# Dealing the opening of RWKV pairs 2 and 3 out over the chain of pairs 0 and 1, decode softmax in parts, first weights in half slabs

## The reference, cut to what matters

```
h  = LN(ALPHA*x + 0.5*swiglu_a(x))
proj = h @ w_in          # q, k, v of differential attention; r, k, v, decay, rate, gate of RWKV-7
attention: p = softmax(q1 k1) - lam*softmax(q2 k2);  o_da = rmsnorm(p @ v)
rwkv (8 heads of 64): S = S*w + (S @ -kk) b' + v k';  o = S @ r   # a scan over the tokens
o_rw = (groupnorm(o) + sum(r*k*r_k)*v) * gate
h2 = LN(ALPHA*h + [o_da, o_rw] @ w_out)
y  = LN(ALPHA*h2 + 0.5*swiglu_b(h2))
```

## Time and profile before

| | us |
|---|---|
| median of 3 runs | 1348.41 (1346.65 to 1348.88) |
| profiled execution, its own time | 1350.16 |
| its span, first to last instruction | 1348.4 |
| mean granted TensorE clock | 0.976 of full |
| TensorE busy | 1255.0 (93%) |
| VectorE busy | 571.8 (42%) |
| ScalarE busy | 426.2 (32%) |
| GpSimd busy | 105.6 (8%) |
| data moved | 174.77 MB, mean 130 GB/s |

### The profile page before, as it was taken

One profiled execution on the slowest core, in us unless ns is written; L12 is line 12 of the kernel. 1 busy time (PEld: TensorE's weight loads), 2 busy tenths in 40 slices (PEclk: granted clock), 3 DMA queues, 4 the chain that ended last, 5 costly groups with the idle time before them and its releaser, 6 DMA issues.

```text
span 1348.4 us, 29923 instructions
## 1 busy us (share of the span) xinstructions
PE 1255.0 (93%) x12840; PEld 1137.5 (84%) x12840; DVE 571.8 (42%) x814; ACT 426.2 (32%) x652; POOL 105.6 (8%) x98
## 2 busy tenths in 40 slices
PE   6999999999998999997788988798999999999995
PEld 6999999999988988874456544487999999999994
DVE  3323233232436445344543643688533232322354
ACT  4222223222324324425532322423322222222222
POOL 0000000000200100010441021013000000000020
PEclk9999999999999999998997999899999999999998
DMA  5222222233223657554463689441222222222221
GB/s 221 94 84 83 86 89 93 66 90 102 87 100 119 269 177 259 166 186 141 145 213 130 208 285 304 156 166 63 95 94 93 93 93 85 77 71 87 87 63 64
DMA packets 55971, 174.77 MB, mean 130 GB/s; under 512 B 7105, under 2 KB 7362, under 8 KB 47298
## 3 DMA queue, kind: packets, MB, share of 16 engines
q1 hardware_dynamic: 53282, 168.84, 36.6%
q10 hardware_dynamic: 2592, 4.52, 0.9%
HBM read 163.58 MB, written 9.76 MB: 129 GB/s over the span
## 4 chain that ended last, share of the span: by engine, by line
PE 39%; DVE 7%; ACT 3%; SPq 3%; issue 2%; DMA 1%; POOL 0%; DVEq 0%; ACTq 0%
PE acc L273 27%; PE acc L296 3%; SPq L2189 2%; PE acc L1343 1%; PE acc L1526 1%; PE acc L1534 1%; SPq L2181 1%; DVE weights_lo L256 1%; PE acc L889 1%; PE acc L1511 1%; PE acc L1280 1%; DVE y_sum L605 1%; PE acc L1321 1%; ACT map L1461 1%; PE acc L1417 1%
## 5 line engine op out<-in xcount | busy, mean ns | idle before, releaser
L256 DVE TENSOR_TENSOR weights_lo<-weights_raw,weights_hi 128x1024 fp32r<-128x1024 f32 (+2 forms) x186 | 210.9, 1136 | 540.1 <-ACT weights_hi L249 540.0
L273 PE MATMUL acc<-x_hi,weights_hi 128*128 128x260 f32 x1696 | 345.3, 285 | 11.6 <-DVE x_lo L2305 11.6
L249 ACT ACTIVATE weights_hi<-weights_raw 128x1024 fp32r<-128x1024 f32 (+2 forms) x186 | 179.5, 967 | 549.1 <-PE acc L273 524.4
L273 PE MATMUL acc<-x_hi,weights_lo 128*128 128x260 f32 x1696 | 342.7, 284 | 0.0
L273 PE MATMUL acc<-x_lo,weights_hi 128*128 128x260 f32 x1696 | 342.1, 283 | 0.0
L273 PEld LDWEIGHTS acc<-x_hi,weights_hi 128*128 128x128 f32 x1696 | 262.9, 189 | 23.7 <-issue 23.3
L273 PEld LDWEIGHTS acc<-x_hi,weights_lo 128*128 128x128 f32 x1696 | 262.4, 189 | 0.0
L273 PEld LDWEIGHTS acc<-x_lo,weights_hi 128*128 128x128 f32 x1696 | 261.9, 189 | 0.0
L273 PE MATMUL acc<-hidden_hi,weights_hi 128*128 128x260 f32 x704 | 143.1, 284 | 0.0
L273 PE MATMUL acc<-hidden_hi,weights_lo 128*128 128x260 f32 x704 | 141.7, 283 | 0.0
L273 PE MATMUL acc<-hidden_lo,weights_hi 128*128 128x260 f32 x704 | 141.6, 283 | 0.0
(11 more groups left out here) (314 smaller groups left out, 1359.4 us busy)
## 6 DMA issues: line engine op xcount, KB each, us to landing
cache_pages<-in_cache_k SPq DMA_DIRECT2D x128, 256.0 KB, 3.5
weights_raw<-in_gate_up_a SPq DMA_DIRECT2D x22, 1024.0 KB, 4.8
weights_raw<-in_gate_up_b SPq DMA_DIRECT2D x22, 1024.0 KB, 4.8
cache_pages<-in_cache_v SPq DMA_DIRECT2D x64, 256.0 KB, 3.8
weights_raw<-in_w_in SPq DMA_DIRECT2D x13, 1024.0 KB, 5.6
projected<-in_cache_v SPq DMA_DIRECT2D x48, 256.0 KB, 3.6
weights_raw<-in_down_a SPq DMA_DIRECT2D x8, 768.0 KB, 4.1
weights_raw<-in_down_b SPq DMA_DIRECT2D x8, 768.0 KB, 4.1
```

Of the source, the lines that this page charges most:

```text
L249: nc.scalar.activation(WH[pr.slot(k)][:, 0:nk, :], RAW[slot][:, 0:nk, P * (k % 2):P * (k % 2) + P], ACT.Copy).then_inc(split_hi, 1)
L256: nc.vector.tensor_tensor(WL[pr.slot(k)][:, 0:nk, :], RAW[slot][:, 0:nk, P * (k % 2):P * (k % 2) + P], WH[pr.slot(k)][:, 0:nk, :].bitcast( ...
L273: mm = nc.tensor.matmul(acc[s][:, a, 0:HALF], w[slot][:, t, :], x[:, k0 + t, HALF * a:HALF * a + HALF], start=begins and t == tiles[0] and ...
```

## The change

Start: the host lays the first block out slab by slab; SyncE loads its two slabs as two transfers and the next block only once all of x is in. x comes in parts of 1, 1, 2, 2, 2 chunks. ScalarE first does a copy of one column (with the table load), then x chunk 0, slab 0, the other chunks, slab 1. The vectors are loaded by SyncE. TensorE makes six products of 512 columns on constants before its first real one.

Middle: spreads and token turns of pairs 2 and 3 leave the second phase's opening and stand between the state steps of pairs 0 and 1, before the late products and behind them. The maximum of the decode softmax is taken per quarter (three quarters in solve, the last behind step 1), the exponential in two halves (behind steps 2 and 3), the sums behind step 4, the turned weights behind steps 5, 6 and 7. The state load of pairs 2 and 3 goes behind the centred copies. The copy of the last key logits goes ahead of the out copies.

```diff
+        X_PARTS = ((0, 1), (1, 2), (2, 4), (4, 6), (6, 8))
+        HALVES = [RAW[0][:, 4 * n:4 * n + 4, :].rearrange("p k (a n) -> p (k a) n", n=P) for n in range(2)]
...
+        OPENED_AT = {1: (("tokB", 2), ("tokK", 2)), 2: (("tokV", 2), ("tokA", 2)), 3: (("tokB", 3), ("tokK", 3)),
+                     4: (("tokV", 3), ("tokA", 3)), 5: (("TT", 2),), 6: (("TT", 3),), 7: (("MT", 2),),
+                     "before": (("T", 2), ("MT", 3)),
+                     "behind": (("T", 3), ("RBT", 2), ("RKT", 2), ("RBT", 3), ("RKT", 3))}
...
         def opening_tensor(pe, two, before):
+            if not before:
...
+                return
             for i in before:
                 centered_tensor(pe, i)
+            decode(pe)
             for i in before:
                 bonus_tensor(pe, i)
+            decode(pe)
+            sums_tensor(pe, before)
...
-        def chain_tensor(pe, two):
+        def chain_tensor(pe, two, nxt):
...
                 if n == 4:
                     step_tensor(pe, b, 2)
-                if n == 6 and a == 0:
-                    decode_weights_tensor(pe)
+                if nxt:
+                    for name in OPENED_AT[n]:
+                        opened_tensor(pe, name)
+                    if n >= 5:
+                        decode_weights_tensor(pe, n - 5)
+            if nxt:
+                for name in OPENED_AT["before"]:
+                    opened_tensor(pe, name)
             for i in two:
                 name = ("late", i)
...
+            if nxt:
+                for name in OPENED_AT["behind"]:
+                    opened_tensor(pe, name)
+                    if name[0] == "RKT":
+                        decode(pe)
...
+        def chain_scalar(act):
+            for n in range(1, 5):
+                for name in OPENED_AT[n]:
+                    token_scalar(act, name)
+                if n in (2, 3):
+                    decode_exp_scalar(act, n - 2)
+            decode_weights_scalar(act)
...
         def chain_vector(dve, two, nxt):
...
-                if a == 0 and n == 3:
-                    decode_max_vector(dve)
-                if a == 0 and n == 5:
-                    decode_sums_vector(dve)
+                if nxt and n == 1:
+                    decode_max_vector(dve, 3)
                 if n == 4:
                     step_out_vector(dve, b)
+                    if nxt:
+                        decode_sums_vector(dve)
                     bonus_terms_vector(dve, b)
+                if nxt and n >= 5:
+                    for name in OPENED_AT[n]:
+                        opened_vector(dve, name)
...
-            stream(up_a, by_pair(gu_a))
+            first = gu_a[0, :, :].rearrange("p (s k n) -> p s k n", s=2, k=DC)
+            sp.dma_start(HALVES[0], first[:, 0, :, :]).then_inc(g("first_raw"), 16)
+            sp.wait_ge(x_loaded[2], 16)
+            sp.dma_start(HALVES[1], first[:, 1, :, :]).then_inc(raw_ready[0], 16)
+            sp.dma_start(VEC[:, :], vecs).then_inc(tables_in, 16)
+            sp.wait_ge(x_loaded[-1], 16)
+            sp.dma_start(RAW[1][:, :, :], by_pair(gu_a)(0, 1)).then_inc(raw_ready[1], 16)
...
             pe.wait_ge(consts_set, 6)
+            for n in range(6):
+                nc.tensor.matmul(acc[3][:, n % 2, :], MEAN[:, :], MEAN[:, 0:1].broadcast_to([P, 512]), start=True, stop=True)
             gate_up_tensor(pe, up_a, 0)
```

More of the change, by code:

```diff
@@ L1614, in step_tensor, with opened_tensor @@
             ring_full(nc.tensor.matmul(one(name), const(C_HEAD), VB if part == 1 else PD, start=True, stop=True))
-        def opening_tensor(pe, two, before):
[L1617 to L1623, removed]
+        def opened_tensor(pe, name):
+            kind, i = name
+            u = i % 2
+            pe.wait_ge(g("features"), 4 if name == ("tokA", 2) else i + 1)
+            if kind == "tokV":
+                was_shifted(pe, 20 + i)
+            if kind in ("RBT", "RKT"):
+                pe.wait_ge(g("r_weighted"), i + 1)
+            if kind == "tokA":
+                turned_crossed(pe, name, FA[u])
+            elif kind in ("tokB", "tokK", "tokV"):
+                turned(pe, name, {"tokB": FB[u], "tokK": FK[u], "tokV": pj(20 + i)[:, 0:SEQ]}[kind])
+            else:
+                lhs, rhs = {"TT": (FB[u], FA[u]), "T": (FA[u], FB[u]), "MT": (FK[u], FA[u]),
+                            "RBT": (FB[u], FR[i]), "RKT": (FK[u], FR[i])}[kind]
+                spread(pe, name, lhs, rhs)
@@ L1624, in opening_tensor @@
+        def opening_tensor(pe, two, before):
+            if not before:
+                for i in two:
+                    for n in ("TT", "T"):
+                        opened_tensor(pe, (n, i))
+                for i in two:
+                    for n in ("tokA", "tokB", "tokK", "tokV"):
+                        opened_tensor(pe, (n, i))
                     decode(pe)
+                for i in two:
+                    for n in ("MT", "RBT", "RKT"):
+                        opened_tensor(pe, (n, i))
+                return
@@ L1740, in chain_tensor @@
                     ring_full(mm)
-                if a and n < 6:
+                if not nxt and n < 6:
                     decode(pe)
@@ L1866, in phase_scalar @@
                 act.dma_start(LATE[:, :], consts[:, NCONST:NCONST + NLATE]).then_inc(g("late_in"), 16)
-            load_states(act, two)
+            if not before:
+                load_states(act, two)
             opening_scalar(act, two, before)
@@ L1870, in phase_scalar @@
             solve_scalar(act, two, nxt)
-            if not before:
-                decode_logits_scalar(act, 3)
-                decode_exp_scalar(act)
-                decode_weights_scalar(act)
+            if nxt:
+                chain_scalar(act)
             states_scalar(act, two)
@@ L2048, in solve_vector @@
                 keys_taken_vector(dve, nxt[1])
+                for q in range(3):
+                    decode_max_vector(dve, q)
             for i in two:
@@ L2306, in _ @@
                                         ALU.subtract).then_inc(x_ready, 1)
+                if c == 0:
+                    first_low(dve, 0)
+            first_low(dve, 1)
+            for k in range(2, 4):
+                split_low(dve, up_a, 0, k)
             dve.wait_ge(tables_in, 16)
-            for k in range(1, 4):
-                split_low(dve, up_a, 0, k)
             gate_up(gate_up_vector, dve, up_a, 0, dn_a)
```

154 lines of the change are left out of this document (90 added, 64 removed).

## The result

The changed kernel takes 1341.45 us (median of 20 runs, 1332.56 to 1350.19) against 1348.64 for the kernel before (20 runs): ratio 0.9947, 95% interval 0.9931 to 0.9962. It gains 7.2 us; 14.9 were predicted. The time lies inside the wide range of the prediction (1328 to 1342), the gain is just under half of the forecast. That it stands on the number of rival (a), 1341.3, is chance: the experiments speak against that rival's mechanism. The profiled execution took 1338.06 with a span of 1336.2; it is 3.4 under its median, the one of before 1.5 above its own. So the two profiles differ by 12.1 and the medians by 7.2: a first warning that two single profiles overstate this change.

The account below looks back on a forecast made before the run. TensorE was taken as the bound (busy 1255.0 of 1348.4 us), with time to win only where it idles or runs slow. Start 4.5 plus middle 10.4 gave 14.9 off 1348.41: 1333.5 us, own range 1330 to 1338, wide range 1328 to 1342.

Parts of the forecast that it names:

- rival (a): Levels: the page stream takes the gain back, only 2.6 us of the middle kept, 1341.3 us; chance 0.1.
- The start's mechanism and size: First slab: starts at 9.6 us, runs at full clock, ends at 15.4 instead of 19.9; gain 4.5 us.
- All 4.5 reach the end: Behind the start: the FFN runs with TensorE always busy, so the start's whole 4.5 us is kept.
- The idle of the middle: Chain and opening of the middle: fillers between state steps leave 3.1 us of 8.0 us TensorE idle.
- TensorE waits some 0.4: Chain, state steps 4 to 5: TensorE has other work during VectorE's three pieces and waits only some 0.4 us.
- The clock of the middle: Chain and opening: two stretches of 4 us at half clock, costing 4.0 us together instead of 9.5.
- Levels and pages at nothing: Behind the opening: gain of 0 to 2 us set against page waits growing by 0 to 2.
- Rival (b): Middle: state steps stand still behind the fillers, all 8.0 us of idle stay, 1338.4 us; chance 0.13.
- Rival (c): Middle: the clock is given back at once, by the skill's rule, 1330.4 us; chance 0.15.
- Rival (d): Middle: the clock stays at half all through the packed stretch, slower at 1359.0 us; chance 0.05.

Follow-up runs that it names:

- e1: Kernel before with only the start part of the change; 1346.48 us, ratio 0.9988.
- e13: e1 with the constant products of e8 (norms 0 and 1, last inverses, output projection); 1342.15 us, ratio 0.9954.
- e2: Kernel before with only the middle part of the change; 1341.31 us, ratio 0.9929.
- e9: Kernel before with only the decode softmax in parts, spreads and token turns staying in the opening; 1347.31 us, ratio 0.9983.
- e11: Kernel before with only a quarter of each value page transferred; 1344.69 us, ratio 0.9967.
- e8: Kernel before plus constant products behind norms 0 and 1, before the last inverses and the output projection, none in the chain; 1345.86 us, ratio 0.9982.
- e4: Changed kernel with softmax sums and bonus terms behind later state steps, turned weights one step later; 1341.86 us, ratio 0.9948.
- e6: Changed kernel without the six warm-up products; 1341.80 us, ratio 0.9947.
- e10: Changed kernel with only a quarter of each value page transferred; 1340.38 us, ratio 0.9929.
- e14: e7 without its two constant products at state step 5 of the chain; 1342.27 us, ratio 0.9953.
- e3: Changed kernel plus two 512-column constant products in TensorE's gap at state step 5; 1340.54 us, ratio 0.9935.
- e7: e3 plus constant products behind norms 0 and 1, before the last inverses and the output projection; 1335.54 us, ratio 0.9901.
- e12: e7 plus one constant product ahead of the first turn of the second levels; 1337.15 us, ratio 0.9914.

## Why the prediction was wrong

**The start's mechanism and size: right at its place.** First product 8.99 (forecast 9.0 to 10.3), slab done at 15.31 (15.4). Ahead of the input projection the ten profiles with the warm-up stand at 403.7, the five with the old start at 407.5: 3.8 kept. The pair shown, 408.2 and 403.6, overstates it: of the five old starts, the one that the prediction read had its clock up last (at 17.4, the others at 14.4 to 16.1).

**"All 4.5 reach the end": not borne out.** The sum carried the gain through stages whose clock it held fixed. e1 keeps 2.5 (its ratio allows at most 3.5), e13, with fillers, 3.7. The clock behind the first norm is a candidate for the difference: full in the profile of before, low in e1's (2.6 us there). It is not shown: three of the four other profiles with the old start (e2, e9, e11) lose 1.5 us there too, and over whole runs e1 loses no more clock than before.

**The idle of the middle: right in what is removed.** Old order: 8.0, 9.5, 9.4, 9.4, 8.9 us idle in chain and opening (before, e1, e8, e11, e13), 9.0 on the mean. New order without a filler in the chain: 4.1, 3.7, 4.9, 3.9, 4.6, 5.5 (after, e2, e4, e6, e10, e14), 4.5 on the mean. 4.6 removed, 4.9 forecast. Luck helped: 4.5 stayed where 3.1 were forecast, but the old order had 9.0 and not 8.0. Inside it "TensorE waits some 0.4" behind the sums was 2.16: the walk had the three VectorE pieces (1.4 + 1.4 + 0.75) about right (3.6 us from 705.90 to 709.54), but put spread TT 2 and the first turned weights beside them. TT 2 takes a pair of ring banks, and by the order of jobs one of the pair holds pair 0's state step 5, which VectorE reads only behind its three pieces (PE L1529 started at 709.87, released by L2148). The turned weights stand behind TT 2.

**The clock of the middle: the step that failed.** The sum let the loss go from 9.5 to 4.0 us, a gain of 5.5. The busy time shows what became of it: 37.9 us on the mean of the five old profiles, 36.4 of the six new ones, so 1.4 gained. Over whole runs the loss fell by about 3 (from 30.3 to 30.9 down to 27.9). Both ends of the term were off.

The old end: the profile of before was the worst of its five (busy 39.1 at 0.75; the others 37.0 to 38.2 at 0.82 to 0.85). With 30 to 31 us of work at full clock instead of 29.5, the old loss is 7 to 8 us, not 9.5. In before the clock fell right at the first state step (703.6); in e1, e8, e11 and e13, with the same order, it fell only 7.6 to 9.2 us behind it.

The new end: the clock did not begin low in after, e4, e6 and e14, as the forecast had it from the one profile. It fell 12 to 14 us behind the first step and stayed at half for 13.6 us in after and 17.0 in e14, not for two times 4; these 4 us were read from no row. (In e2 it was low at the beginning too, from 702.3 to 709.1, and again from 715.9.) By 30 to 31 us of work the new loss is 5.4 to 6.4 us.

That the full clock can be had is shown: in the three profiles with the gap filled (e3, e7, e12) the stretch is 36.0, 36.0 and 37.3 us at 0.99 to 1.00. That this is near the forecast's 36.6 is chance: it holds 2.0 of filler and no loss, the forecast 4.0 of loss. Why the clock stays up in e10 without filler is open, and so why it fell in e4.

Together: 2.5 for the start and 4.6 + 1.4 for the middle make 8.5, beside 7.2 measured (7.3 to 8.2 against the kernel before in the other sets). Of the 6.4 us between this and the 14.9 of the forecast, 4.1 are the clock of the middle, 2.0 the start and 0.3 the idle time.

**Levels and pages at nothing: right in sum.** Levels and solve take 88.5, 87.2, 87.2, 85.3 us in before, e1, e8, e13 (mean 87.1) and 86.0, 86.5, 86.4, 87.7 in after, e2, e4, e6 (mean 86.7). In e3, e7, e12 and e14 they take 88.8 to 91.2 at a clock of 0.94 to 0.98, though the code of the levels is that of after but for one product in e12. So some levels also lose clock, and what decides it is open. Rival (a) fell: the waits for pages did not grow, and light pages (e10, e11) did not drive the kernels apart. The stream does cost: with light pages the levels are 81.2 and 83.3.

**Rival (b)** (steps stand still behind the fillers, 8.0 idle stays) fell by the same idle times, though its place, VectorE between steps 4 and 5, is where the gap was. **Rival (c)**, the clock given back at once: not in after, where the clock stayed at half for 13.5 us with TensorE busy 13.13. The trace of after speaks against the rule quoted from the Trainium skill, "TensorE: Matmul & The Clock Gate", section "What's actually happening", as that of before did. **Rival (d)** fell: in after spreads and turns ran at full clock up to 711.9 and from 727.2, and the mean over the stretch was 0.83.

## What to carry to other kernels

Price each stage's clock from several profiles of the same code, not from one, since the same chain showed 0.75 and 0.85, and check it against the mean clock over all runs. Where a short gap stands ahead of dense small products, a few products on constants in it (2.0 us here) can be worth more than moving the wait; here they brought 0.9 and 6.7 us in two comparisons. Look for the in-order engine that gets three duties between two steps of a recurrence.

## What the runs showed of the hardware

The granted clock decides most of the scatter: the fastest run of after took 1332.56 us at 0.985, the slowest 1350.19 at 0.974; that is 20 and 35 us lost to the clock, 15 of the 17.6 between them. The clock can stay at half while TensorE is busy nearly all the time: 13.13 of 13.50 us in after, mostly in products of 64 columns. The same chain with the same 2.16 us gap fell to half clock in five of six profiles and not in the sixth (e10). The clock column is no guide at the very start: it says 1.00 in the earlier trace rows while instructions take 0.216 us, and in after, behind the warm-up, they take 0.13 (6.32 us for 48, with a short wait). Less traffic also shortened the levels beyond the waits that the profile names: those of the old order went from 87.1 us (mean of four profiles) to 81.2 (one profile, e11). TensorE's idle time in them went from 10.7 (before) to 5.3, 5.4 less, where its visible waits for pages had been 3.9.
